# A streaming encoder layer: keys and queries projected first, attention laid between the gate's and u's projections, output weights asked for early

## The chip, the core and the metric

One core of one Trainium2 chip. The time is the device time of one execution in microseconds. The core's engines are TensorE (PE in the rows, matmuls; PEld is its weight load), VectorE (DVE), ScalarE (ACT), GpSimd (POOL) and SyncE (SP, which here only asks for weights). Each runs its own list of instructions in order, and they meet at semaphores.

## The reference

Two layers over 512 prompt rows and 64 sample rows, width 1024. Cut to what the change touches:

```python
h = x @ w_in                       # columns q 512 | k 128 | v 128 | u 512 | gv 512
q, k = rope(q, pos), rope(k, pos)
att_o = sink_attention(q, k, v, sinks, mask)            # window of 64-row chunks c-2, c-1, c
vn = layer_norm(gelu(gv)) per group; s = tril(w_s[g]) @ vn + b[g]
gm_o = gelu(u) * s                                      # over 128 positions, 4 groups
mixed = concat([rms_norm(att_o), rms_norm(gm_o)])
x = layer_norm(ALPHA * x + mixed @ w_o)
x = layer_norm(ALPHA * x + grouped_moe(x))              # 16 experts, top 2, for each row
```

## The kernel before, in words

All rows lie in five tiles of 128 (`NT = 5`; tile 4 is the sample, padded). Every large product is a sum of three passes, high part by high, high by low, low by high. A weight comes as a unit of 512 rows by 512 columns (1 MB; a unit of keys and values has 256 columns) into one of four slots of `raw`; ScalarE writes its high part (`split_hi`), VectorE the low part (`split_lo`), and a product waits for the latter. `unit s` stands in slot `s % 4`. The same pair of steps makes high and low parts of everything turned on TensorE: rows (`xt`), queries (`qt`), keys (`kt`), mixed rows (`mt`).

One layer runs: (1) the head: for each tile turn x, then project the gate's values gv; (2) projections of keys and values, of q, of u, each over all five tiles; (3) attention, gMLP and the product with w_o in a software pipeline over `t` (a loop of eight steps: scores of tile t, weighted values of tile t-1, the turn of mixed rows of t-2, output and layer norm of t-3); (4) the routing; (5) sixteen experts, whose weights stream at the pace of the DMA; (6) a tail that adds the experts' rows and normalises, within which the head of layer 1 stands. The layer loop turns behind that head.

The order is written out by hand, once for each engine. `fill_plan` (line 60) gives each PSUM result its bank and its turn in that bank; a writer waits (`wait_free`) until the turn before was read. `scores`, `gmlp`, `weighted_values`, `turn_mixed`, `output`, `turn_x1` are TensorE's steps; VectorE's are `rotate` (rope), `scores_out` (scale, mask, row maxima), `attention_out`, `gmlp_out`, `rms_norm`, `mixed_lo`, `mixed_out`, `layer_norm`; ScalarE's are `gelu`, `exponentials`, `probs_out` (copy of turned probabilities), `sums_of_squares`, `mixed_hi`, `router_rows_out`. A change of function on ScalarE between gelu, exp and sqrt brings an `ACT_TABLE_LOAD`.

Of the kernel before, what the change touches and what calls it, by code (L numbers as in the profile page):

```python
# [64 lines left out]
def fill_plan():  # L65
# [17 lines left out]
    fill(("qt", 0), "G")  # L83
    fill("kt1", "F")
    fill("wst", "H")
    for t in range(NT + 3):
        if t < NT:
            for j in range(4):
                fill(("s", t, j), "ABCD"[j])
        if t + 1 < NT:  # L90
            fill(("qt", t + 1), "H")
        if t == 0:
            for r in range(NT):
                fill(("gm", r), "GH"[r % 2])
        if 4 <= t < NT + 2:
            fill(("logit", t - 4), "H")
            fill(("turned logit", t - 4), "H")
        if t >= 3:
            for c in range(2):
                fill(("wo", c, t - 3), "AB"[c])  # L100
        if 1 <= t < NT + 1:
            for j in range(4):
                fill(("pt", t - 1, j), "EF"[j % 2])
            fill(("o", t - 1), "G")
        if 2 <= t < NT + 2:
            for h in range(2):
                fill(("mt", t - 2, h), "EF"[h])
        if 3 <= t < NT + 1:
            for h in range(2):
                fill(("rt", t - 3, h), "CD"[h])  # L110
    for t in (NT - 2, NT - 1):
# [14 lines left out]
def build(nc, x_prompt, x_sample, cache_k, cache_v, w_in, sinks, gm_ln_g, gm_ln_b, gm_ws, gm_bs,  # L126
# [5 lines left out]
    with ctx:  # L132
# [10 lines left out]

        raw = sb("raw", [P, RB, 4, HALF])
        w_hi = sb("w_hi", [P, RB, 4, HALF], F32R)
        w_lo = sb("w_lo", [P, RB, 4, HALF], F32R)
        x = sb("x", [P, NT, D])
# [7 lines left out]
        small = sb("small", [P, 400])  # L155
# [6 lines left out]
        xt_hi = over(base_t, "xt_hi", [P, KT_N, ROWS], F32R)  # L162
        xt_lo = over(base_t, "xt_lo", [P, KT_N, ROWS], F32R, 4 * KT_N * ROWS)
        keys_hi = over(base_t, "keys_hi", [P, 7 * P], F32R)
        keys_lo = over(base_t, "keys_lo", [P, 7 * P], F32R, at=3584)
        q_hi = over(base_t, "q_hi", [P, 4, P], F32R, at=7168)
        q_lo = over(base_t, "q_lo", [P, 4, P], F32R, at=9216)
        probs = over(base_t, "probs", [P, 2, 4, 2, 256], at=11264)
        probs_t = over(base_t, "probs_t", [P, 2, 4, P], at=27648)
        mask = over(base_t, "mask", [P, 3, 256], at=31744)  # L170
        ws_t = over(base_t, "ws_t", [P, 4, P], at=34816)
        consts = over(base_t, "consts", [P, 3 * P + 46 + 8 * NT])
        x1_t = over(base_t, "x1_t", [P, KT_N, P], at=36864)

        logits_t = over(base_t, "logits_t", [NE, P], at=3584)
# [9 lines left out]
        mt_hi = over(base_m, "mt_hi", [P, KT_N, P], F32R, at=2 * QB)  # L185
        mt_lo = over(base_m, "mt_lo", [P, KT_N, P], F32R, at=2 * QB + 4 * D)
        squares = over(base_m, "squares", [P, HALF], at=2 * QB + 8 * D)
# [31 lines left out]
        w12, warm = sm(NT, 2), sm(3)  # L219

# [19 lines left out]
        in_slot = over(base_t, "in_slot", [P, ON_CHIP, 2 * NT, P], BF16, at=11264)  # L240
# [32 lines left out]
        ws_in, mask_in, consts_in = sem("ws_in"), sem("mask_in"), sem("consts_in")  # L273
# [76 lines left out]
        def width(s):  # L350
            return 256 if s in (2, 3) else HALF
# [84 lines left out]
        def _(sp):  # L436
# [33 lines left out]
            with sp.Fori(0, DEPTH) as l:  # L470
                s = 0
                for c0, n in ((1280, HALF), (HALF, 256), (0, HALF), (768, HALF)):
# [3 lines left out]
                for c in range(2):  # L476
                    for k in range(2):
# [205 lines left out]
        def _(act):  # L683
# [24 lines left out]
            with act.Fori(0, DEPTH) as l:  # L708
# [6 lines left out]
                for t in range(4):  # L715
                    gelu(0, gv, t)
# [1144 lines left out]
```

## Time and profile before

| | us |
|---|---|
| median of three runs (1278.83 to 1288.0) | 1281.9 |
| profiled execution | 1284.19 |
| its span, first to last instruction | 1282.4 |
| granted TensorE clock, mean | 0.927 |
| PE busy in the span | 1062.2 (83%) |
| VectorE busy | 905.1 (71%) |
| ScalarE busy | 709.7 (55%) |

The profile's page cuts the span into 40 slices. TensorE's row of them shows nines for the projections (35 to 120 us, and 650 to 740 us in layer 1), sevens to nines in the attention stage, a gap at the routing, then nines through the experts, in which the DMA row also stands at nine. A "stretch" below is a span of time in this execution, in us from its start; "granted clock" 1.00 is 2.4 GHz and 0.5 is 1.2 GHz, so 0.97 says that 6% of the stretch ran at the lower level.

### The profile page before, as it was taken

Reading aid. Unit: us, or ns where it says so; the run is one execution under the profiler, and the core shown is the slowest. Engines: PE = TensorE matmul, PEld = TensorE weight load, DVE = VectorE, ACT = ScalarE, POOL = GpSimd, SP = SyncE. Lnnn points to the kernel's source line nnn. Section 1 sums busy time; section 2 is a strip of 40 time slices with the busy share of each in tenths; the row PEclk is TensorE's granted clock in tenths of the full one; section 3 lists DMA queues with packets and bytes.
Section 4 is the critical chain, followed back from the end, with each engine's and each line's share of the span. In section 5 each row is a group of like instructions: output and inputs, shape, how many; then the busy total and the mean of one; then the engine's idle time right before and its main releaser. Section 6 shows DMA issues by size and latency. Waiting matters only on the chain.

```text
span 1282.4 us, 16627 instructions
## 1 busy us (share of the span) xinstructions
PE 1062.2 (83%) x5422; PEld 875.3 (68%) x5422; DVE 905.1 (71%) x1096; ACT 709.7 (55%) x857; POOL 233.5 (18%) x164
## 2 busy tenths in 40 slices
PE   4999789947899999997389977996589999999920
PEld 3887677736777787785278856884477777777810
DVE  2573864568788888985758466636778788888827
ACT  2423663254777777776431267513468677777722
POOL 3000000007122211201440000000541222221015
PEclk9999999968999999999589988998689999999975
DMA  9422100026999999996713202102389999999751
GB/s 292 140 72 99 67 34 25 33 83 208 348 359 355 374 365 370 383 366 246 276 51 139 86 13 83 41 17 99 107 307 361 360 355 381 369 358 369 282 192 57
DMA packets 115620, 273.24 MB, mean 213 GB/s; under 512 B 10016, under 2 KB 13056, under 8 KB 114400
## 3 DMA queue, kind: packets, MB, share of 16 engines
q1 hardware_dynamic: 98608, 227.36, 49.8%
q0 software_dynamic: 14336, 33.00, 7.2%
q10 hardware_dynamic: 2608, 12.06, 2.6%
q8 instruction: 33, 0.54, 0.2%
q14 instruction: 35, 0.29, 0.1%
HBM read 262.00 MB, written 25.22 MB: 224 GB/s over the span
## 4 chain that ended last, share of the span: by engine, by line
PE 39%; DMA 17%; DVE 16%; issue 13%; ACT 8%; POOL 3%; DVEq 2%; POOLq 1%; ACTq 0%; SPq 0%
DMA raw<-in_w_gate 14%; PE bankA L1494 8%; PE bankB L1494 8%; DVE w_lo L385 5%; PE bankC L1494 4%; ACT w_hi L379 4%; PE bankD L1494 3%; PE bankA L1706 3%; PE bankB L1706 3%; POOL slot_rows L608 2%; DVE xt_lo L400 2%; PE bankC L1729 2%; DMA rows<-x_rows,cur_src 2%; PE bankD L1729 2%; PE bankE L1483 1%
## 5 line engine op out<-in xcount | busy, mean ns | idle before, releaser
L385 DVE TENSOR_TENSOR w_lo<-raw,w_hi 128x2048 fp32r<-128x2048 f32 x216 | 487.5, 2268 | 114.9 <-ACT w_hi L379 113.4
L379 ACT ACTIVATE w_hi<-raw 128x2048 fp32r<-128x2048 f32 x216 | 409.7, 1901 | 218.1 <-DMA raw<-in_w_down 60.9
L1706 PE MATMUL bankA<-w_hi,xt_hi 128*128 128x512 f32 x256 | 103.8, 405 | 18.8 <-DVE xt_lo L400 18.1
L1706 PE MATMUL bankB<-w_hi,xt_hi 128*128 128x512 f32 x256 | 102.8, 401 | 0.0
L1706 PE MATMUL bankA<-w_lo,xt_hi 128*128 128x512 f32 x256 | 101.0, 394 | 0.0
L1706 PE MATMUL bankA<-w_hi,xt_lo 128*128 128x512 f32 x256 | 100.9, 394 | 0.0
L1706 PE MATMUL bankB<-w_hi,xt_lo 128*128 128x512 f32 x256 | 100.1, 391 | 0.0
L1706 PE MATMUL bankB<-w_lo,xt_hi 128*128 128x512 f32 x256 | 99.7, 390 | 0.0
L594 POOL DMA_INDIRECT y_rows<-expert_out,idx x32 | 55.3, 1728 | 216.4 <-ACT expert_out L859 216.4
L588 POOL DMA_INDIRECT rows<-x_rows,idx x24 | 46.0, 1917 | 248.7 <-PE bankF L1483 233.0
L1706 PEld LDWEIGHTS bankA<-w_hi,xt_hi 128*128 128x128 f32 x256 | 48.8, 190 | 38.6 <-issue 29.2
L395 ACT ACTIVATE xt_hi<-bankE 128x512 fp32r<-128x512 f32 x42 | 24.6, 585 | 68.2 <-PE bankE L1483 68.2
L1729 PE MATMUL bankC<-w_hi,xt_hi 128*128 128x512 f32 x128 | 53.6, 419 | 3.8 <-DVE xt_lo L400 3.8
L1706 PEld LDWEIGHTS bankA<-w_hi,xt_lo 128*128 128x128 f32 x256 | 48.8, 190 | 10.6
L1706 PEld LDWEIGHTS bankB<-w_hi,xt_lo 128*128 128x128 f32 x256 | 48.0, 188 | 10.7
L1706 PEld LDWEIGHTS bankA<-w_lo,xt_hi 128*128 128x128 f32 x256 | 48.8, 191 | 9.4
L400 DVE TENSOR_TENSOR xt_lo<-bankE,xt_hi 128x512 fp32r<-128x512 f32 x42 | 28.8, 685 | 36.9 <-ACT xt_hi L395 36.9
L1706 PEld LDWEIGHTS bankB<-w_lo,xt_hi 128*128 128x128 f32 x256 | 48.2, 188 | 9.3
L1706 PEld LDWEIGHTS bankB<-w_hi,xt_hi 128*128 128x128 f32 x256 | 48.1, 188 | 9.1
L1729 PE MATMUL bankC<-w_hi,xt_lo 128*128 128x512 f32 x128 | 51.1, 399 | 0.0
L1729 PE MATMUL bankC<-w_lo,xt_hi 128*128 128x512 f32 x128 | 50.8, 397 | 0.0
L1729 PE MATMUL bankD<-w_hi,xt_hi 128*128 128x512 f32 x128 | 50.4, 394 | 0.0
(321 smaller groups left out, 2479.1 us busy)
## 6 DMA issues: line engine op xcount, KB each, us to landing
raw<-in_w_gate SPq DMA_DIRECT2D x64, 1024.0 KB, 8.1
raw<-in_w_up SPq DMA_DIRECT2D x64, 1024.0 KB, 7.8
raw<-in_w_down SPq DMA_DIRECT2D x64, 1024.0 KB, 7.3
raw<-in_w_in SPq DMA_DIRECT2D x12, 1024.0 KB, 8.0
raw<-in_w_o SPq DMA_DIRECT2D x8, 1024.0 KB, 5.3
y_rows<-y_rows ACTq DMA_DIRECT2D x8, 1024.0 KB, 8.3
x_rows<-x POOLq DMA_DIRECT2D x10, 512.0 KB, 3.0
raw<-in_w_in SPq DMA_DIRECT2D x4, 512.0 KB, 8.2
```

Source lines behind the costliest of these rows:

```text
L379: act.activation(w_hi[:, s % RB, :, 0:n], raw[:, s % RB, :, 0:n], ACT.Copy).then_inc(hi_done, 1)
L385: dve.tensor_tensor(w_lo[:, s % RB, :, 0:n], raw[:, s % RB, :, 0:n], w_hi[:, s % RB, :, 0:n].bitcast(F32), ALU.subtract).then_inc(lo_done, 1)
L395: act.activation(dst, bank_of(name)[:, :].rearrange("p (k n) -> p k n", k=4), ACT.Copy).then_inc(s, 1)
L400: read(dve.tensor_tensor(lo, bank_of(name)[:, :].rearrange("p (k n) -> p k n", k=4), hi.bitcast(F32), ALU.subtract), name)
L588: pool.indirect_dma_start(out=rows[:, e % 2, :], out_offset=None, in_=x1_dram, in_offset=bass.IndirectOffsetOnAxis(ap=src.bitcast(U32), ax ...
L594: pool.indirect_dma_start(out=y2_dram, out_offset=bass.IndirectOffsetOnAxis(ap=idx[:, e, 0:1].bitcast(U32), axis=0), in_=expert_out[:, e % ...
L608: pool.indirect_dma_start(out=slot_dram, out_offset=bass.IndirectOffsetOnAxis(ap=slots[:, c:c + 1].bitcast(U32), axis=0), in_=ints[:, c, : ...
L1483: ins = pe.transpose(bank_of(name)[:, k * P:(k + 1) * P], src, ident)
L1494: ins = pe.matmul(out, a[:, k, col:col + P], w[:, slot, j, 0:n], start=(m == 0 and a is a_hi and w is w_hi), stop=(m == len(steps) - 1 and ...
L1706: ins = pe.matmul(out, a[:, 4 * k + t, (c % 2) * P:(c % 2 + 1) * P], w[:, (s + k) % RB, t, :], start=(k == t == 0 and a is xt_hi and w is ...
L1729: ins = pe.matmul(bank_of(f"down{h}")[:, :], a[:, 2 * j + r, cols], w[:, (s + j) % RB, 2 * r + h, :], start=(j == r == 0 and a is xt_hi an ...
```

## The change

- `w_in` is taken in the order keys and values, q, gate, u. The head of each layer projects keys, values and q tile by tile (it projected gv before). The banks of these projections rotate over six (A, B, C, D, G, H).
- Each projection and each output product can be issued in two halves of four row blocks, so other work stands between them. In five rounds t = 0 to 4 TensorE does gate(t), scores(t), u(t), and the weighted values of tile t-1, in pieces (`half_product`, `turn_probs`, `values`). gMLP goes by tile, not by group: `gmlp(t)` are four 128-column products.
- ScalarE and VectorE get orders written out to match: gelu, exponentials and copies of probabilities alternate in each round; the spreads of the gate's norm come in three lots (`gate_spread`, `gate_scale`).
- Scratch moves: the turned x stays until its last projection; probabilities have a buffer for each tile (two lie in raw slots 0 and 1); queries and keys lie in raw slots 2 and 3; mixed rows have two buffers. So the units of `w_o` are asked for when their slot is free: units 8 and 9 behind the turns of tile 0's and tile 1's probabilities, 10 and 11 behind tile 4's scores.
- The mask shrinks to 8 numbers a row, fetched once by six small DMAs at the start instead of one of 393 KB in each layer.

```diff
-    for g in range(4):
-        for t in range(NT):
-            fill(("proj", g, t), "ABCD"[(g * NT + t) % 4])
+    for t in range(NT):
+        for g in range(2):
+            fill(("proj", g, t), "ABCDGH"[(2 * t + g) % 6])
...
+                for s, free in ((8, ("pt", 0, 3)), (9, ("pt", 1, 3)), (10, ("s", NT - 1, 3)), (11, ("s", NT - 1, 3))):
+                    wait_filled(sp, free, l)
...
+            for m in range(3):
+                for a in range(2):
+                    pool.dma_start(mask[:, m, 4 * a:4 * a + 4], c_mask[m, :, 0::64], allow_slow_non_contiguous=True).then_inc(boot, 16)
...
@@ ScalarE
+                for t in (2, 3):
+                    gelu(2, gv, t)
+                    probs_out(t - 1, range(4))
+                    gelu(3, u, t)
+                    queries_out(t + 1)
+                    exponentials(t)
+                    gate_spread(2 * t - 4, 2 * t - 2)
...
@@ VectorE
+                for t in range(NT):
+                    keys_out(t)
+                    if t == NT - 1:
+                        split_lo(dve, l, 4)
+                        split_lo(dve, l, 5)
+                    rotated_queries(t)
...
+                gmlp_out(0)
+                gmlp_out(1)
+                scores_out(4)
+                attention_out(2)
+                rms_norm(0)
+                split_lo(dve, l, 8)
+                rms_norm(1)
+                gate_scale(2, 4, 2)
+                gate_norm(2)
+                gate_norm(3)
+                mixed_lo(0)
+                split_lo(dve, l, 9)
...
+                gate_scale(4, NT, 3)
+                gate_norm(4)
+                attention_out(4)
+                rms_norm(2)
+                gmlp_out(4)
+                mixed_out(0)
+                layer_norm(0)
...
@@ TensorE, head
                 for t in range(NT):
-                    if 2 <= t + 1 < NT:
+                    wait_read(pe, ("xt", t, 1), l)
+                    for k in range(2):
+                        projection(l, 0, t, k)
+                    if t in (1, 2):
                         turn_rows(l, t + 1)
...
+                    for k in range(2):
+                        projection(l, 1, t, k)
+                    if t in (0, 2):
+
+                        turn_rows(l, 1 if t == 0 else 4)
...
@@ TensorE, rounds
+                            turn_probs(t - 1, (0, 1))
+                            projection(l, 3, t, 0)
+                            values(t - 1, 0)
+                            values(t - 1, 1)
+                            turn_probs(t - 1, (2, 3))
+                            if t == NT - 1:
+                                turn_mixed(0)
+                            projection(l, 3, t, 1)
+                            values(t - 1, 2)
+                            values(t - 1, 3)
...
+                output(0, 0)
+                gmlp(2)
+                gmlp(3)
+                attention_end(NT - 1)
+                turn_mixed(1)
+                output(0, 1)
+                gmlp(4)
+                for t in range(1, NT):
+                    output(t, 0)
+                    if t + 1 < NT:
+                        turn_mixed(t + 1)
```

First place, TensorE at the weighted values. Before, in tile 1's (bank E and F take turned probabilities, G the values; `kv` are keys and values, `probs_t` the turned probabilities):

```order
L1483 MATMUL bankE<-ident,probs 128x128 x4
L1537 REGISTER_ALU
L1483 MATMUL bankF<-ident,probs 128x128 x4
L324 REGISTER_ALU
L328 REGISTER_ALU
L1559 MATMUL bankG<-kv,probs_t 128x64 x4
L1537 REGISTER_ALU
L1483 MATMUL bankE<-ident,probs 128x128 x4
L1559 MATMUL bankG<-kv,probs_t 128x64 x4
L1537 REGISTER_ALU
L1483 MATMUL bankF<-ident,probs 128x128 x4
L328 REGISTER_ALU
```

After, in tile 2's (`probs_57` is that tile's buffer, bank B the product of u of tile 3, `xt` the turned rows):

```order
L1538 MATMUL bankB<-w_lo,xt 128x512
L1538 MATMUL bankB<-w_hi,xt 128x512
L332 REGISTER_ALU
L336 REGISTER_ALU
L1596 MATMUL bankG<-kv,probs_t 128x64 x8
L1577 REGISTER_ALU
L1525 MATMUL bankE<-ident,probs_57 128x128 x4
L1577 REGISTER_ALU
L1525 MATMUL bankF<-ident,probs_57 128x128 x4
L1538 MATMUL bankB<-w_hi,xt 128x512
L1538 MATMUL bankB<-w_lo,xt 128x512
```

A value product that stood right behind a turn now has half a projection of u ahead of it, and the next half behind it.

Second place, VectorE ahead of the first output product, which waits for the low part of tile 0's mixed rows (`mt_lo`, after: `mt_70`). Before:

```order
L1124 RECIPROCAL small<-small 128x2
L1127 SCALAR_TENSOR_TENSOR q<-q,small,table 128x512
L1127 SCALAR_TENSOR_TENSOR u<-u,small,table 128x512
L1074 REGISTER_ALU
L1075 TENSOR_TENSOR small<-small 128x8
L1077 RECIPROCAL small<-small 128x8
L320 REGISTER_ALU
L1080 TENSOR_TENSOR q<-bankG,small 128x512
L399 ISA
L400 TENSOR_TENSOR mt_lo<-bankE,mt_hi 128x512
L399 REGISTER_ALU
L400 TENSOR_TENSOR mt_lo<-bankF,mt_hi 128x512
```

After (`gv` rows are the gate's norm of tiles 2 and 3):

```order
L1131 SCALAR_TENSOR_TENSOR u<-u,small,table 128x512
L1081 RECIPROCAL small<-small 128x8
L1073 TENSOR_SCALAR gv<-gv,small 128x128 x4
L1075 TENSOR_TENSOR gv<-gv,table 128x512
L1077 TENSOR_TENSOR gv<-gv,table 128x512
L1073 TENSOR_SCALAR gv<-gv,small 128x128 x4
L1075 TENSOR_TENSOR gv<-gv,table 128x512
L1077 TENSOR_TENSOR gv<-gv,table 128x512
L407 ISA
L408 TENSOR_TENSOR mt_70<-bankE,mt_70 128x512
L407 REGISTER_ALU
L408 TENSOR_TENSOR mt_70<-bankF,mt_70 128x512
```

The low part stood behind an attention output; now it stands behind the gate's norm of two tiles, and a `w_lo` split stands a little further ahead.

Third place, VectorE behind the head. Before (the last low parts of turned x, then the statistics of gv; the branch is the layer loop's start):

```order
L400 TENSOR_TENSOR xt_lo<-bankE,xt_hi 128x4x128
L400 TENSOR_TENSOR xt_lo<-bankF,xt_hi 128x4x128
L400 TENSOR_TENSOR xt_lo<-bankE,xt_hi 128x4x128
L400 TENSOR_TENSOR xt_lo<-bankF,xt_hi 128x4x128
L385 TENSOR_TENSOR w_lo<-raw,w_hi 128x4x256 x2
L1027 UNCONDITIONAL_BRANCH
L1027 ISA
L1033 BN_STATS small<-gv 128x6 x16
```

After (keys, then queries, of tile 0; bank A and B are wanted again by the projections of tile 3):

```order
L408 TENSOR_TENSOR xt<-bankE,xt 128x512
L408 TENSOR_TENSOR xt<-bankF,xt 128x512
L408 TENSOR_TENSOR xt<-bankE,xt 128x512
L408 TENSOR_TENSOR xt<-bankF,xt 128x512
L1045 UNCONDITIONAL_BRANCH
L1045 ISA
L1050 COPY kv<-bankA 128x128
L1010 TENSOR_TENSOR rope_a<-bankA,rope 128x128
L1012 TENSOR_TENSOR rope_b<-bankA,rope 128x2x32
L1013 TENSOR_TENSOR rope_b<-bankA,rope 128x2x32
L1021 TENSOR_TENSOR kv<-rope_a,rope_b 128x128
L1010 TENSOR_TENSOR rope_a<-bankB,rope 128x512
```

The first reader of a projection's bank is now VectorE behind the last turned tile and behind the loop's start; it was ScalarE (gelu).

## Rows read from the trace of the kernel before

**Rows 1.** Stretches: length, busy time of each engine, then granted clock, DMA share, GB/s.

```profile
95.15:259.34 164.19, 146.47 (x867) 122.45 (x866) 92.19 (x152) 74.13 (x178) 4.56 (x8) 0.97 0.14 50
713.35:878.94 165.59, 147.05 (x868) 122.25 (x867) 92.02 (x152) 74.12 (x178) 4.57 (x8) 0.96 0.14 50
122.36:165.71 43.35, 30.33 (x232) 25.43 (x230) 32.68 (x53) 31.00 (x86) 0.74 (x1) 0.92 0.20 71
```

**Rows 2.** TensorE's waits, 95 to 262: us in total, times, longest.

```profile
PE bankG L1559 <- ACT probs_t L746: 5.3, 6, 4.0
```

**Rows 3.** TensorE in order of time, 53 to 80: start, us, operation.

```profile
53.53 0.28 PE L1494 MATMUL bankB<-w_hi,xt_hi 128*128 128x256 f32 x1
...
56.40 0.28 PE L1494 MATMUL bankC<-w_hi,xt_hi 128*128 128x256 f32 x1
...
67.92 0.40 PE L1494 MATMUL bankC<-w_hi,xt_hi 128*128 128x512 f32 x1
...
73.39 0.39 PE L1494 MATMUL bankD<-w_hi,xt_hi 128*128 128x512 f32 x1
```

**Rows 4.** TensorE, 152 to 208: as before, in brackets the idle time and its releaser.

```profile
152.70 1.20 PE L1559 MATMUL bankG<-kv,probs_t 128*128 128x64 f32 x8 [4.03 <-ACT probs_t L746]
...
186.47 0.38 PE L1577 MATMUL bankA<-keys_hi,q_hi 64*128 64x256 f32 x1
...
188.43 1.92 PE L1617 MATMUL bankH<-x_t,wrt 128*16 128x128 f32 x16
190.28 0.50 PE L1494 MATMUL bankA<-w_hi,mt_hi 128*128 128x512 f32 x1
...
201.59 0.65 PE L1483 MATMUL bankE<-ident,probs 128*128 128x128 f32 x4
...
207.39 0.61 PE L1483 MATMUL bankE<-ident,q 128*128 128x128 f32 x4
```

**Rows 5.** VectorE in order of time, 97 to 157.

```profile
97.40 1.11 DVE L1064 TENSOR_SCALAR gv<-gv,small 128x128 f32<-128x128 f32 x4
98.58 0.69 DVE L1066 TENSOR_TENSOR gv<-gv,table 128x512 f32<-128x512 f32 x1
...
99.96 4.49 DVE L385 TENSOR_TENSOR w_lo<-raw,w_hi 128x2048 fp32r<-128x2048 f32 x2
...
150.55 0.68 DVE L1093 SCALAR_TENSOR_TENSOR probs<-bankA,mask 128x512 f32<-128x512 f32 x1
...
153.12 2.29 DVE L1098 TENSOR_REDUCE small<-probs 128x8 f32<-128x2048 f32 x1
...
156.72 0.75 DVE L1127 SCALAR_TENSOR_TENSOR q<-q,small,table 128x512 f32<-128x512 f32 x1
```

**Rows 6.** ScalarE in order of time, 157 to 175.

```profile
157.20 0.60 ACT L746 ACTIVATE probs_t<-bankF 128x512 f32<-128x512 f32 x1 [1.82 <-PE bankF L1483]
157.81 1.28 ACT L753 ACT_TABLE_LOAD   x1
...
170.42 0.51 ACT L753 ACTIVATE probs<-probs,small 128x256 f32<-128x256 f32 x1 [1.37 <-DVE small L1103]
...
174.38 0.19 ACT L755 ACTIVATE small<-small 128x8 f32<-128x8 f32 x1
```

**Rows 7.** TensorE, the first projection of layer 0.

```profile
18.95 0.77 PE L1494 MATMUL bankA<-w_hi,xt_hi 128*128 128x512 f32 x1 [11.70 <-issue]
```

**Rows 8.** TensorE, the head of layer 1.

```profile
629.70 0.79 PE L1494 MATMUL bankA<-w_hi,xt_hi 128*128 128x512 f32 x1 [6.05 <-DVE xt_lo L400]
...
645.05 1.11 PE L1483 MATMUL bankE<-ident,x 128*128 128x128 f32 x4 [5.95 <-POOL x L668]
```

**Rows 9.** ScalarE at the turn of the layer loop.

```profile
664.21 1.28 ACT L712 ACT_TABLE_LOAD   x1 [3.02 <-issue]
```

**Rows 10.** GpSimd, the small strided fetch of the gMLP bias.

```profile
26.84 0.75 POOL L551 DMA_DIRECT2D small<-in_gm_bs  x1
```

**Rows 11.** The page, its DMA issues: times asked for, size, us to landing.

```profile
raw<-in_w_o SPq DMA_DIRECT2D x8, 1024.0 KB, 5.3
```

More of the change, by code:

```diff
@@ new lines, in _ @@
+                gelu(3, u, 1)
+                probs_out(0, range(4))
+                queries_out(2)
+                exponentials(1)
+                for t in (2, 3):
[5 more added lines that the diff above has]
+                    gate_spread(2 * t - 4, 2 * t - 2)
+                sums_of_squares(0)
+                sums_of_squares(1)
+                probs_out(3, range(2))
@@ new lines, in _ @@
+                split_hi(act, l, 8)
+                gelu(2, gv, 4)
+                probs_out(3, range(2, 4))
+                mixed_hi(0)
+                split_hi(act, l, 9)
+                gelu(3, u, 4)
+                split_hi(act, l, 10)
+                exponentials(4)
+                split_hi(act, l, 11)
+                probs_out(4, range(4))
+                mixed_hi(1)
+                gate_spread(4, NT)
+                sums_of_squares(2)
+                sums_of_squares(3)
+                row_spread(0)
@@ new lines, in _ @@
+                gate_stats(0)
+                scores_out(0)
+                queries_lo_out(1)
+                for t in range(1, 4):
+                    scores_out(t)
+                    if t >= 2:
+                        attention_out(t - 2)
+                    gate_stats(t)
+                    if t == 3:
+                        gate_scale(0, 2, 1)
+                        gate_norm(0)
+                        gate_norm(1)
+                    queries_lo_out(t + 1)
+                gmlp_out(0)
@@ new lines, in _ @@
+                gmlp_out(1)
[9 more added lines that the diff above has]
+                split_lo(dve, l, 9)
+                gate_stats(4)
+                attention_out(3)
+                split_lo(dve, l, 10)
+                gmlp_out(2)
+                gmlp_out(3)
@@ new lines, in _ @@
+                split_lo(dve, l, 11)
+                mixed_lo(1)
+                gate_scale(4, NT, 3)
[5 more added lines that the diff above has]
+                layer_norm(0)
+                mixed_lo(2)
+                rms_norm(3)
+                mixed_out(1)
+                layer_norm(1)
+                mixed_lo(3)
+                expert_logits_out(0)
+                rms_norm(4)
@@ L1213, in _ @@
+                mixed_out(2)
+                logits_out(0)
+                layer_norm(2)
+                mixed_lo(4)
+                expert_logits_out(1)
+                mixed_out(3)
+                logits_out(1)
+                layer_norm(3)
+                expert_logits_out(2)
+                mixed_out(4)
+                logits_out(2)
+                layer_norm(4)
                 expert_logits_out(NT - 2)
@@ new lines, in _ @@
+                gmlp(2)
[4 more added lines that the diff above has]
+                gmlp(4)
+                for t in range(1, NT):
+                    output(t, 0)
+                    if t + 1 < NT:
+                        turn_mixed(t + 1)
+                    if t >= 2:
+                        expert_logits(t - 2)
+                    output(t, 1)
+                    turn_x1(t - 1)
+                    if t >= 2:
+                        turn_logits(t - 2)
@@ L1764, in turned, with three_pass @@
                         ins.then_inc(ov_pe, 1)
-                    def three_pass(out, col, units, after):
+                    def three_pass(out, n, units, after):
                         pe.wait_ge(ov_dve, ran * DVE_STEPS + after)
```

522 lines of the change are left out of this document (233 added, 289 removed).

## The prediction

> **What bounds the kernel now.** I read the slices of the page first: the experts run at the DMA's pace and are not touched, so what a layer gains ahead of its routing is passed on to the end. Then, by stretches, the part of each layer from the first projection of u (95.15; 713.35) to the end of tile 4's output product (259.34; 878.94). In the first, 164.2 us, PE is busy 146.5 and idle 17.7; the granted clock is 0.97, so 0.03 x 164.2 = 4.9 us of its work went to the lower level, and the work at 2.4 GHz is 141.6. In layer 1: 165.6, idle 18.5, 0.04 x 165.6 = 6.6 lost, work 140.4 [rows 1]. VectorE has 92 and ScalarE 74 us there. So PE has the most work, but it is not continuous: in the stretch 122 to 166, behind the projections, it is busy 30.3 of 43.4 at clock 0.92 [rows 1], because scores, row maxima, exponentials, copies and values follow each other with nothing laid between. The waits say whose: 5.3 us of them are for the copies of probabilities, one alone 4.0 [rows 2]. The view in order of time shows PE idle 4.03 us ahead of tile 1's values [rows 4]. About 22.6 and 25.1 us a layer (idle and clock) are all that this part can give.
>
> **The change, part by part.** I follow each engine's new list with durations of before. Prices: half a projection 5.47 / 2 = 2.7; keys and values of a tile 2.9 [rows 3]; scores of a tile 1.96, router product 1.85, values of a tile with their four turns 5.8, of which a pair of turns 0.9 [rows 4]; VectorE: the gate's norm of a tile 1.1 + 2 x 0.76 = 2.7, a weight's low part 2.25, scores out 4 x 0.6 + 2.3 + 0.6 = 5.3, `rms_norm` 1.6 [rows 5]; ScalarE: table load 1.28, exponentials of a tile 174.38 + 0.19 - 170.42 = 4.15, a copy 0.6 [rows 6]. Time 0 is the start of gate(0).
>
> *Round 0*, to 14.9. ScalarE must write the keys' high parts behind unit 7's low part (7.1); scores(0) start at 9.8, as PE arrives. No stall.
>
> *Round 1*, to 34.7. scores(1) wait for the low part of queries 1, which VectorE has behind scores_out(0) and its maxima: 1.4 us. The values of tile 0 still stand right behind their turns, and the copies behind the gelu of u(1): 2.4. Sum 3.8.
>
> *Rounds 2 and 3*, to 53.4 and 73.9 (with two gMLP products). Here the idea works: turned probabilities are copied while half a u projection runs (first place in the order). The tight chain is ScalarE's behind `turn_queries`: copy 0.6, load and exp 5.4, load and sqrt 1.6, load and gelu 1.9, two copies 1.1 = 10.6, against PE's 2.7 + 1.0 + 2.7 + 1.0 + 0.9 + 2.7 = 11.0 ahead of the values. It holds by 0.4, so I take no stall.
>
> *Round 4*, to 94.6. `turn_mixed(0)` needs a bank that ScalarE empties behind a weight split (1.9) and a gelu with its load (1.9): stall 1.6.
>
> *First output product.* It needs tile 0's low mixed rows. VectorE does scores_out(4) to 85.0, attention_out 1.1, rms_norm 1.7, a weight 2.3, rms_norm 1.7, the norm of two tiles 5.6, then mixed_lo: done 98.7 (second place). Stall 4.2. Tile 4's values follow with 1.2 of stall.
>
> *Second output product of tile 1's row.* `output(1, 0)` wants bank A, which mixed_out(0) reads behind gate_norm(4), attention_out(4), rms_norm(2), gmlp_out(4): VectorE gets there at 123.7, PE at 120.2. Stall 3.5. From there PE needs 5.5 + 0.9 + 1.9 + 5.5 + 0.9 + 0.2 = 14.9 a tile and VectorE about 11, so PE sets the pace to the end.
>
> Stalls together 3.8 + 1.6 + 4.2 + 1.2 + 3.5 = 14.3, less 0.6 where a piece's modelled end already covers them: 13.7. The work is 141.6 + 5 x 5.47 for gv = 168.9 in layer 0 and 167.7 in layer 1. On the clock's loss: it was 4.9 for 17.7 idle, 6.6 for 18.5; in proportion 3.8 and 4.9. My stalls are mostly shorter and stand between long products, so I take 2 and 3; the proportional value is the other end. Adding full pieces one by one gives 2 to 3 us less work than the busy time (its ends overlap); I take 2 off. New part: 168.9 + 13.7 + 2 - 2 = 182.6, and 182.4. Before, with gv: 164.2 + 27.3 = 191.5, and 192.9. Gains 8.9 and 10.5.
>
> *Heads.* Before, layer 0 went from 18.95 [rows 7] to 95.15. The first keys unit has half the bytes and half the splitting, so PE starts near 11; but q(0) needs units 2 and 3, 3 MB in rather than 2, and ends near 25. Then comes what the change adds: keys of tile 3 want bank A, which VectorE reads behind the low part of tile 4's x (third place): 2.6 us. By steps of 8.35 a tile, u would start at 94.0 instead of 95.15: gain 1. Bounds -3 to +5. Layer 1 is now paced by the tail: PE waits 6.05 and 5.95 for rows [rows 8], and q(0) fills the second wait (+5); but q(2)'s turn of tile 4, then the loop's start, for which ScalarE needed 3.0 us [rows 9], stand ahead of the keys' read: stall 4.7 and some clock. Result -1, bounds -5 to +4. Together 0.
>
> *At the end of the part* VectorE copies a turned logit ahead of the last layer norm, which waits for PE's turns behind the last product: 0.6 a layer, 1.2.
>
> *Weights of w_o.* Units 10 and 11 are asked for at 81, split from 94 and 101 on ScalarE, used from 113; such a unit lands in 5.3 us [rows 11]. Cover of some 8 us; were it gone, each us would be one of PE. Experts' first units are asked for from 90 on and used 90 us later. *Mask.* Six strided fetches like the gMLP bias, 0.75 us of issue each [rows 10], 4.5 on POOL ahead of releasing x tiles 2 to 4; turn_rows(2) stands near 31 and the release near 26. Nothing. Layouts, mask by broadcast, buffers: the same element counts, nothing (bounds +-1).
>
> Sum: -8.9 - 10.5 + 0 + 1.2 = -18.2. I have counted only the waits I could see in five lists, and a list followed misses waits, never work; for those I add 2 us a layer (one more wait like those for queries). So -14.2. The profiled execution took 1284.2, of which 1282.4 is its span; the median of the runs is 2.3 below it, 1281.9. The change is the same against each, so the span goes to 1268.2, the profiled execution to 1270.0 and the median to **1268**.
>
> **A rule weighed against the trace.** In each round ScalarE changes between gelu, exp and sqrt, up to three loads, where before one tile had at most two. The rows show a load of 1.28 us that starts 0.01 us behind the copy ahead of it [rows 6]: nothing else is paid. The Trainium skill (ScalarE: Activation LUTs, What ACT_TABLE_LOAD costs) states about 2.66 us for a switch, with a drain. By the rule the chain of rounds 2 to 4 would grow by 3 x 1.38 = 4.1 and stand 3.7 over PE's; three rounds, two layers: +22, so about 1290. It is part of rival 3.
>
> **Rivals.**
> 1. *The hand-offs are hidden better.* The 4.2 and 3.5 stalls shrink (VectorE can gain on me wherever I let it wait), no clock is lost and nothing unseen comes. Gain 8.9 + 10.5 + about 4 a layer + heads 3 = 30: 1252. For it: VectorE's 92 us of 165. Against: VectorE works through from 81 to 124 in my list without a gap.
> 2. *VectorE's queue is later than I have it.* Both stalls double (+7.7 a layer): it decides if one of the four weight splits there waits for ScalarE, whose exp(4) stands between them. 1268 + 15 = 1283: no change.
> 3. *Slower: ScalarE paces the rounds.* Place: probs_out behind exp, sqrt and gelu. Price: if its chain is 3.5 us longer than 10.6 (late maxima, or the rule above), PE stalls 3.1 in rounds 2, 3, 4 of both layers, 19 us, and after such waits it ran values at the lower clock before (1.20 for eight, [rows 4]): 1.5 each, 9. That is 1268 + 28 = 1296. It decides from about 3 us on. Against: loads show no drain, and maxima are ready 5 us ahead of exp.
>
> **How the numbers follow.** Forecast 0.45, its own range 1260 to 1276; rival 1 0.24; rival 2 0.19; rival 3 0.12 (0.03 of it the rule). 1% of 1281.9, about what can be told from no change here, is 12.8: faster means under 1269.1. Of the forecast's range a little over half lies below. Faster: 0.25 + 0.24 = 0.49; same 0.20 + 0.19 = 0.39; slower 0.12. The range leaves out 0.08 of rival 1's low end and all of rival 3: 1249 to 1286.
>
> **What would show it.** Right: no PE wait for `probs_t` over 1 us in rounds 2 and 3; a wait of about 4 us for `mt` low parts ahead of the first output product and of 3 to 4 for bank A; about 182 us from gate(0) to tile 4's last output in both layers; a wait of 2 to 6 us in the fourth tile of each head. Wrong: waits for probabilities in every round (rival 3); experts that don't start earlier by what the part gains.

## The result, and the profile after

The changed kernel takes 1290.95 us (median of 20 runs) beside 1282.95 for the kernel before: ratio 1.0061, interval 1.0041 to 1.0080. It is slower by 0.6%; I had forecast 1268, and 1286 as the upper end of the range. The profiled execution took 1288.56, its span 1287.0, granted clock 0.924.

The stretches of the changed kernel that answer to [rows 1] start at the first projection of gate(0), since the gate now belongs to this part (columns: length, busy time of each engine with the number of instructions, granted clock, DMA share, GB/s). The first two are the parts of the two layers, the next four lie inside the first part, the last two in the head of layer 1:

```profile
65.26:260.82 195.56, 181.22 (x1010) 150.04 (x1011) 116.64 (x233) 88.49 (x192) 5.32 (x10) 0.96 0.18 63
692.54:885.43 192.89, 178.30 (x1010) 147.40 (x1011) 115.04 (x233) 88.46 (x192) 4.57 (x8) 0.96 0.18 63
126.91:135.30 8.39, 8.39 (x51) 6.56 (x50) 2.23 (x4) 8.03 (x22) 0.00 (x0) 1.00 0.00 0
142.45:151.56 9.11, 9.11 (x59) 8.34 (x58) 5.23 (x14) 3.28 (x5) 0.00 (x0) 0.81 0.00 0
177.29:184.39 7.10, 7.10 (x26) 5.80 (x27) 6.29 (x13) 6.00 (x19) 0.00 (x0) 0.79 0.42 148
202.98:210.38 7.40, 7.40 (x26) 5.88 (x27) 5.47 (x8) 0.29 (x1) 0.48 (x1) 0.77 0.24 73
630.87:692.54 61.67, 52.54 (x273) 46.84 (x273) 41.35 (x74) 17.95 (x20) 23.04 (x21) 0.86 0.20 64
673.20:678.68 5.48, 5.48 (x25) 5.48 (x26) 4.74 (x14) 0.00 (x0) 0.00 (x0) 0.51 0.00 0
```

I predicted 182.6 and 182.4 for the first two; they are 195.6 and 192.9. The idle time in them, 14.3 and 14.6, is close to my 13.7. The busy time is not.

TensorE's waits in layer 0's part (total, times, longest), which answer to [rows 2]:

```profile
PE bankG L1596 <- DVE q L1092: 4.4, 3, 1.5
PE bankA L1538 <- DVE x L1140: 3.2, 1, 3.2
PE bankC L1615 <- DVE q_lo L408: 2.6, 2, 1.3
PE bankA L1538 <- DVE mt L408: 2.0, 1, 2.0
PE bankE L1525 <- ACT ws_t L802: 1.2, 1, 1.2
PE bankG L1596 <- ACT probs_t L737: 1.0, 4, 0.2
```

What the change was to remove is removed: the wait for copied probabilities was 5.3 with one of 4.0, and is 1.0 in four pieces. The largest wait is one that stands nowhere in my prediction. TensorE, then VectorE, in round 3 of the changed kernel in order of time (start, us, operation, in brackets the idle time and its releaser):

```profile
140.62 1.99 PE L1596 MATMUL bankG<-kv,probs_t 128*128 128x64 f32 x16 [1.47 <-DVE q L1092]
```

```profile
136.44 2.29 DVE L1108 TENSOR_REDUCE small<-probs 128x8 f32<-128x2048 f32 x1
...
139.45 0.20 DVE L1089 RECIPROCAL small<-small 128x8 f32<-128x8 f32 x1
139.80 0.69 DVE L1092 TENSOR_TENSOR q<-bankG,small 128x512 f32<-128x512 f32 x1
```

The values of tile 2 go to bank G, which still holds those of tile 1. Its reader, `attention_out(1)`, stands on VectorE behind `scores_out(3)` with its row maxima (2.29 us), and ends at 140.5. This happens in rounds 2, 3 and 4, with waits of 1.48, 1.47 and 1.46.

### The profile page after: what moved, and what is told of

It reads as the page before. It is cut to its first block, busy times and chain, and to the rows that moved or that the text cites. A ratio compares the mean times of both kernels' runs of the same rounds, so it can differ in the third digit from the quotient of the medians.

```text
span 1287.0 us, 17033 instructions
## 1 busy us (share of the span) xinstructions
PE 1074.2 (83%) x5470; PEld 885.9 (69%) x5470; DVE 909.9 (71%) x1124; ACT 717.4 (56%) x865; POOL 242.5 (19%) x170
## 4 chain that ended last, share of the span: by engine, by line
PE 33%; DMA 21%; DVE 20%; issue 12%; ACT 6%; DVEq 3%; POOL 2%; POOLq 1%; ACTq 1%; SPq 0%
DMA raw<-in_w_gate 16%; PE bankA L1538 9%; DVE w_lo L393 7%; PE bankB L1538 7%; ACT w_hi L387 5%; DVE xt L408 3%; PE bankG L1596 2%; DVE small L1108 1%; PE bankE L1525 1%; PE bankD L1538 1%; DVE x L1464 1%; PE bankC L1799 1%; POOL slot_rows L621 1%; PE bankA L1776 1%; PE bankD L1799 1%
## 5 line engine op out<-in xcount | busy, mean ns | idle before, releaser
L393 DVE TENSOR_TENSOR w_lo<-raw,w_hi 128x2048 fp32r<-128x2048 f32 (+1 forms) x216 | 487.8, 2268 | 107.9 <-ACT w_hi L387 106.7
L387 ACT ACTIVATE w_hi<-raw 128x2048 fp32r<-128x2048 f32 (+1 forms) x216 | 409.8, 1901 | 179.8 <-DMA raw<-in_w_gate 60.3
L1776 PE MATMUL bankA<-w_hi,xt 128*128 128x512 f32 x512 | 167.6, 398 | 22.1 <-DVE xt L408 22.1
L1776 PE MATMUL bankB<-w_hi,xt 128*128 128x512 f32 x512 | 166.3, 396 | 0.0
L1776 PEld LDWEIGHTS bankA<-w_hi,xt 128*128 128x128 f32 x512 | 97.0, 189 | 52.4 <-issue 32.6
L1776 PEld LDWEIGHTS bankB<-w_hi,xt 128*128 128x128 f32 x512 | 96.2, 188 | 19.5
L1776 PE MATMUL bankA<-w_lo,xt 128*128 128x512 f32 x256 | 100.3, 392 | 0.0
L1776 PE MATMUL bankB<-w_lo,xt 128*128 128x512 f32 x256 | 99.8, 390 | 0.0
L1799 PE MATMUL bankC<-w_hi,xt 128*128 128x512 f32 x256 | 93.6, 407 | 3.3 <-DVE xt L408 3.3
L1799 PE MATMUL bankD<-w_hi,xt 128*128 128x512 f32 x256 | 90.0, 392 | 0.0
L1538 PE MATMUL bankB<-w_hi,xt 128*128 128x512 f32 x224 | 75.9, 404 | 1.5 <-DVE w_lo L393 1.4
L1538 PEld LDWEIGHTS bankA<-w_hi,xt 128*128 128x128 f32 x224 | 46.1, 218 | 26.0 <-issue 10.0
```

The costliest lines, as they stand in the source:

```text
L387: act.activation(w_hi[:, s % RB, :, 0:n], raw[:, s % RB, :, 0:n], ACT.Copy).then_inc(hi_done, 1)
L393: dve.tensor_tensor(w_lo[:, s % RB, :, 0:n], raw[:, s % RB, :, 0:n], w_hi[:, s % RB, :, 0:n].bitcast(F32), ALU.subtract).then_inc(lo_done, 1)
L1538: ins = pe.matmul(bank_of(name)[:, 0:n], part[:, 4 * k0 + j, :], w[:, s % RB, j, 0:n], start=(k0 == j == 0 and part is hi and w is w_hi), ...
L1776: ins = pe.matmul(out, a[:, c % 2, 4 * k + t, :], w[:, (s + k) % RB, t, :], start=(k == t == 0 and a is xt_hi and w is w_hi), stop=(k == 1 ...
L1799: ins = pe.matmul(bank_of(f"down{h}")[:, :], a[:, n, 2 * j + r, :], w[:, (s + j) % RB, 2 * r + h, :], start=(j == r == 0 and a is xt_hi an ...
```

## Experiments

Each kernel is the changed one with the edit shown. The results, with the span of the profiled execution cut at the same places: start of gate(0) in layer 0, end of tile 4's output product, the first turned x of layer 1 ("head 1" is from there to gate(0) of layer 1), and the output product of layer 1. "Busy" is TensorE's in that part, "end" the time from layer 1's last output product to the end of the span.

| kernel | ratio to before | gate(0) | part 0 / busy | head 1 | part 1 / busy | end |
|---|---|---|---|---|---|---|
| before | 1 | 67.9* | 191.5* | 64.4* | 192.9* | 403.5 |
| changed | 1.0061 (1.0041 to 1.0080) | 65.3 | 195.6 / 181.2 | 68.8 | 192.9 / 178.3 | 401.6 |
| e_oread | 0.9970 (0.9943 to 0.9997) | 65.1 | 186.3 / 174.3 | 66.9 | 188.5 / 177.8 | 398.1 |
| e_mix | 0.9928 (0.9893 to 0.9962) | 65.9 | 184.9 / 174.8 | 66.7 | 183.7 / 174.8 | 400.4 |
| e_head | 1.0013 (0.9978 to 1.0047) | 62.8 | 192.5 / 179.4 | 63.1 | 193.2 / 178.5 | 403.1 |
| e_quarter | 1.0263 (1.0211 to 1.0315) | 67.0 | 202.1 / 186.3 | 67.2 | 206.2 / 190.9 | 395.1 |
| e_all | 0.9788 (0.9747 to 0.9828) | 62.6 | 177.2 / 172.3 | 63.4 | 178.7 / 172.4 | 404.9 |
| e_best | 0.9677 (0.9644 to 0.9711) | 63.3 | 173.3 / 171.8 | 64.7 | 174.3 / 171.9 | 399.6 |
| e_best_q | 0.9757 (0.9727 to 0.9787) | 62.2 | 180.0 / 178.2 | 63.8 | 180.3 / 178.4 | 399.7 |
| e_best_undo | 0.9797 (0.9751 to 0.9843) | 63.5 | 178.5 / 172.6 | 63.0 | 183.4 / 177.3 | 403.7 |

\* with the 27.3 us of the gate's projections counted into the part instead of the head, as in the prediction. The last column is the same code in the changed kernel and all its edits, and yet it goes from 395 to 405 in single executions. The way from the end of part 0 to the first turned x of layer 1, which has no column, goes from 361 to 367 (362 before, 363 in the changed kernel). So I read each edit in its own part and take the total from the ratio. A difference from the changed kernel is the quotient of two ratios, and the interval of e_head touches that of the changed kernel. A part's busy time is that of one execution, which need not be a typical one: that of e_oread took 1267.7 us at a mean clock of 0.930, beside a median of 1278.0 and clocks of 0.923 to 0.927 in the other nine.

### e_oread: the reader of bank G first

```diff
                 for t in range(1, 4):
-                    scores_out(t)
                     if t >= 2:
                         attention_out(t - 2)
+                    scores_out(t)
...
-                scores_out(4)
                 attention_out(2)
+                scores_out(4)
```

> The changed kernel with one thing moved on VectorE: attention_out(t-2) stands ahead of scores_out(t) instead of behind it, for t = 2, 3 and 4. Nothing else. Theory A (waits that my lists missed, and the lower clock behind short waits): in the changed kernel TensorE waits 3 times 1.46 us a layer for the reader of bank G, and the stretch from that wait of round 3 to round 4 ran at a granted clock of 0.81. Gone with the wait: 4.4 of idle and about 2 of clock a layer, so 1291 - 13 = 1278, and the page shows no wait of bank G for q. Theory B (the rounds are paced by VectorE and ScalarE anyway): the wait comes back at another bank in the same round, 1288 to 1291. Theory C (only the idle time comes back, the clock does not): 1291 - 9 = 1282.

Measured: 0.9% less than the changed kernel, about 12 us. No wait for `q` is left, part 0 is 9.3 shorter and part 1 4.4. Theory A holds for the total. The layers show something else as well: busy time falls by 6.9 in layer 0 and by 0.5 in layer 1, with the same instructions, and the wait ahead of the first output product grows from 2.0 to 3.8, since TensorE comes earlier and VectorE does not. How much of the 6.9 belongs to the edit and how much to this execution, whose clock was the highest of the ten, one trace does not tell. Here too the product behind that wait ran at a granted clock of 0.77:

```profile
169.29:176.65 7.36, 7.36 (x26) 5.91 (x27) 6.29 (x13) 4.21 (x12) 0.00 (x0) 0.77 0.39 142
```

### e_mix: VectorE's list around the first output products

```diff
                 gate_norm(2)
-                gate_norm(3)
                 mixed_lo(0)
                 split_lo(dve, l, 9)
+                gate_norm(3)
...
                 split_lo(dve, l, 11)
+                mixed_out(0, (0,))
                 mixed_lo(1)
...
-                mixed_out(0)
+                mixed_out(0, (1,))
                 layer_norm(0)
```

> The changed kernel with VectorE's list changed around the first output products: mixed_lo(0) and the low part of unit 9 stand ahead of gate_norm(3) instead of behind it, and the first half of mixed_out(0), which frees bank A, stands ahead of mixed_lo(1) instead of behind gate_norm(4), attention_out(4), rms_norm(2) and gmlp_out(4). Theory A: the two waits of 2.0 and 3.2 us a layer vanish, and the two output products behind them take 5.7 us each instead of 7.1 and 7.4 (8.0 and 8.3 in layer 1), since they no longer follow a gap: 5.2 + 3.1 = 8.3 in layer 0, 9.7 in layer 1, so 1291 - 18 = 1273. Theory B (VectorE is the limit there): the time is wanted again at gmlp_out, mixed_lo(1) or layer_norm(0), and less than 8 us come back in all: 1283 to 1290.

Measured: 1.3% less than the changed kernel, 17 us; theory A said 18. Of the two waits 0.7 is left of the first and nothing of the second in layer 0, and the output products behind them take 5.7 us:

```profile
PE bankG L1597 <- DVE q L1092: 4.4, 3, 1.5
...
PE bankA L1539 <- DVE mt L408: 0.7, 1, 0.7
```

### e_head: turned rows one product earlier

```diff
                     if t in (1, 2):
-                        turn_rows(l, t + 1)
+                        turn_rows(l, 2 * t)
                     for k in range(2):
                         projection(l, 1, t, k)
-                    if t in (0, 2):
+                    if t in (0, 1):
 
-                        turn_rows(l, 1 if t == 0 else 4)
+                        turn_rows(l, 2 * t + 1)
```

> The changed kernel with TensorE's head changed: tile 3's rows are turned behind q(1) and tile 4's behind keys and values of tile 2, each one product earlier, so that VectorE is through with the turned rows and the loop's start one product earlier. Theory A: in layer 1 the wait of 5.7 us ahead of keys and values of tile 3 goes to 0 to 1, and the products behind it no longer run at a clock of 0.5 (about 2.7 us); in layer 0 the wait of 2.3 goes. Sum 5.2 + 2.7 + 2.3 = 10: 1291 - 10 = 1281. Theory B (the loop's start, some 3.4 us on VectorE and ScalarE, and the rows of the tail set the pace): the wait moves to the turn of tile 4 or to q(3), and no more than 4 come back: 1287 to 1291.

Measured: 0.5% less, 6 us, between the theories, and hardly clear of the noise. The wait ahead of keys and values of tile 3 was, in the changed kernel, TensorE's and VectorE's:

```profile
673.20 0.58 PE L1538 MATMUL bankA<-w_hi,xt 128*128 128x256 f32 x1 [5.73 <-DVE rope_b L1013]
```

```profile
668.30 0.68 DVE L408 TENSOR_TENSOR xt<-bankF,xt 128x512 fp32r<-128x512 f32 x1
672.39 0.29 DVE L1050 COPY kv<-bankA 128x128 f32<-128x128 f32 x1 [3.41 <-issue]
```

With the rows turned earlier 2.1 us of the 5.7 stay. VectorE has the turned rows behind it at 658.83, 6.6 us earlier than in the changed kernel if one counts from the first turned x, but then it stands 5.25 us at the start of the layer loop instead of 3.41, and what it waits for there the trace does not show:

```profile
664.08 0.29 DVE L1050 COPY kv<-bankA 128x128 f32<-128x128 f32 x1 [5.25 <-issue]
```

Head 1 is 5.7 shorter, head 0 2.4: the place is right, 8 of the expected 10 us are seen in the trace, 6 in the ratio.

### e_quarter: the gate's projection in quarters, scores in blocks of six

```diff
-                    projection(l, 2, t, 0)
                     if t:
-                        scores(t, (0, 1))
-                    projection(l, 2, t, 1)
+                        for k in range(2):
+                            projection(l, 2, t, k, (0, 1))
+                            scores(t, (2 * k,))
+                            projection(l, 2, t, k, (2, 3))
+                            scores(t, (2 * k + 1,))
```

> The changed kernel with more changes between work, not more work: in rounds 1 to 4 the gate's projection goes in quarters, and behind each quarter stand the scores of one pair of heads, so that scores come in four blocks of 6 products instead of two of 12. The same products, banks and waits. Read from the changed kernel: between two products of a projection 0.23 us pass, from the last one to the first scores product 0.32, between the first two scores products 0.22 instead of 0.11, from the last to the next projection product 0.21, between that one and its successor 0.31 to 0.34: some 0.4 us for going into a block of scores and out again. Theory A (the change of work costs): 2 more blocks in 4 rounds of 2 layers, 16 x 0.4 = 6.4 us more of TensorE's busy time; 1291 + 6 = 1297. Theory B (the excess over my sum is the clock alone): within 1 us of the changed kernel, 1290 to 1292.

Measured: 2.0% above the changed kernel, 26 us; I had expected 6. My price of a cut was too low. The same round 3, at full clock in both, took 8.39 in the changed kernel (above) and here

```profile
130.37:140.46 10.09, 9.99 (x51) 7.24 (x50) 2.77 (x4) 9.49 (x23) 0.00 (x0) 1.00 0.01 2
```

so 1.70 for two cuts. How it comes about shows in the order of time; the changed kernel, round 3, at the edge between half a projection and a pair of scores:

```profile
129.31 0.39 PE L1538 MATMUL bankA<-w_lo,xt 128*128 128x512 f32 x1
129.53 0.39 PE L1538 MATMUL bankA<-w_hi,xt 128*128 128x512 f32 x1
129.85 0.38 PE L1615 MATMUL bankC<-keys_hi,q_hi 64*128 64x256 f32 x1
130.07 0.28 PE L1615 MATMUL bankC<-keys_lo,q_hi 64*128 64x256 f32 x1
130.19 0.28 PE L1615 MATMUL bankC<-keys_hi,q_lo 64*128 64x256 f32 x1
130.20 0.38 PE L1615 MATMUL bankD<-keys_hi,q_hi 64*128 64x256 f32 x1
...
130.89 0.28 PE L1615 MATMUL bankD<-keys_hi,q_lo 64*128 64x256 f32 x1
131.10 0.50 PE L1538 MATMUL bankA<-w_hi,xt 128*128 128x512 f32 x1
131.44 0.39 PE L1538 MATMUL bankA<-w_lo,xt 128*128 128x512 f32 x1
```

And a block of six in e_quarter, with the product behind it:

```profile
132.10 0.38 PE L1617 MATMUL bankC<-keys_hi,q_hi 64*128 64x256 f32 x1
...
133.00 0.50 PE L1538 MATMUL bankA<-w_hi,xt 128*128 128x512 f32 x1
```

Starts inside the projection are 0.23 apart; at the edges 0.32, 0.22, 0.21 and 0.34. And scores in 64 rows of one bank run beside those of the other (starts 0.01 apart), the second 0.35 behind the first: 12 products in a pair take 1.25, 24 in one block took 1.96 before [rows 4], but 6 alone take 0.9. So the edit does more than cut: a block of six fills one bank and has nothing beside it. Four such blocks take 3.6 where two of twelve take 2.5, which is 1.1 of the 1.70; the other 0.6 is edges. Part 0 grew by 6.5, the size of the added work (6.4, from e_best_q below), part 1 by 13.3, of which 12.6 is busy time: the same 6.4 and about 6 of clock. The two spans differ by only 15 us: the end is 6.5 shorter in this execution, which took 1304.0 where the median of its six runs is 1313.1. Where the rest of the 26 lies no trace shows.

### e_all, e_best: the edits together

e_all is the three edits above. e_best adds the following (`scores_out(0, 1)` takes the low part of queries 1 between tile 0's scores and their maxima):

```diff
@@ VectorE
                 rms_norm(1)
+                mixed_lo(0)
+                split_lo(dve, l, 9)
                 gate_scale(2, 4, 2)
                 gate_norm(2)
-                mixed_lo(0)
-                split_lo(dve, l, 9)
                 gate_norm(3)
-                gate_stats(4)
                 attention_out(3)
+                gate_stats(4)
...
-                scores_out(0)
-                queries_lo_out(1)
+                scores_out(0, 1)
@@ ScalarE
+                probs_out(0, range(2))
                 gelu(3, u, 1)
-                probs_out(0, range(4))
+                probs_out(0, range(2, 4))
@@ TensorE, attention_end(0)
+                    turn_probs(t, (0, 1))
                     if t == 0:
                         wait_read(pe, "wst", l)
                         pe.sem_inc(held_pe, 1)
-                    turn_probs(t, (0, 1))
```

> The three edits together: attention_out ahead of scores_out, mixed_lo(0) and half of mixed_out(0) earlier, rows of tiles 3 and 4 turned one product earlier. Alone they stood at 0.997, 0.993 and 1.001 of the kernel before, against 1.006 of the changed kernel. Theory A (independent waits at different places of one path): the gains of 0.9, 1.3 and 0.5% add up, less about 1.2 us a layer, because without the waits for bank G TensorE comes 4 us earlier to the first output product while VectorE does not (with the first edit alone that wait grew from 2.0 to 3.8): 0.979 + 0.002 = 0.981, about 1259. Theory B (a second limit, the DMA ahead of the experts or VectorE's 92 us in the part, takes over): 0.988 or more, no better than the best single edit by over half a per cent.

> As e_all, and five more moves: mixed_lo(0) and the low part of unit 9 right behind rms_norm(1), ahead of the gate's norm of tiles 2 and 3; attention_out(3) ahead of gate_stats(4); the low part of queries 1 ahead of the maxima of tile 0's scores; on ScalarE two copies of tile 0's probabilities ahead of the gelu of u(1); on TensorE the wait for the spatial weights' copy behind the first turned probabilities. Theory A: the wait ahead of the first output product goes to under 0.5 us (VectorE would be through at the time TensorE arrives), the wait for the low part of queries 1 (1.3) and most of that for ws_t (1.2) go: 1.2 + 1.3 + 0.7 = 3.2 a layer, so 6 us under e_all, 0.976 of the kernel before, about 1252. The two layer parts from gate(0) to tile 4's last output product then take about 180 us each, a little under the 182.6 that I predicted of the changed kernel. Theory B: gate_norm(2) or (3) come too late for gmlp(2) and gmlp(3), and the wait only moves there: no better than e_all.

Measured: e_all 0.979 (expected 0.981), e_best 0.968 (expected 0.976, 1252), at 1241.92 us. The three edits of e_all add up (0.9, 1.3 and 0.5% alone, 2.7% together), so within the noise their waits were independent. The parts of e_best, the two layers, then round 3 and the first output product:

```profile
63.28:236.62 173.34, 171.82 (x1011) 143.95 (x1010) 114.77 (x233) 88.26 (x192) 4.56 (x8) 1.00 0.21 70
666.98:841.28 174.30, 171.90 (x1011) 143.97 (x1010) 115.73 (x233) 88.27 (x192) 4.71 (x9) 1.00 0.20 70
117.59:125.98 8.39, 8.39 (x52) 6.56 (x50) 3.20 (x7) 8.03 (x22) 0.00 (x0) 1.00 0.01 3
159.49:165.23 5.74, 5.74 (x28) 4.76 (x28) 5.37 (x14) 5.71 (x17) 0.00 (x0) 1.00 0.64 208
```

TensorE is busy 171.8 of 173.3 us at full clock. This is the same work as in the changed kernel, where it took 181.2: the difference, 9.4 us, I put down to the lower clock. The granted clock of 0.96 over 195.6 us gives 7.8, and of 0.96 over 192.9 us in layer 1 7.7 where the busy times differ by 6.4, so it is most of the difference, to some 1.5 us. All that TensorE still waits for in part 0:

```profile
PE bankG L1599 <- ACT probs_t L737: 1.3, 4, 0.5
PE bankE L1528 <- ACT probs_t L737: 0.3, 1, 0.3
```

By the parts e_best gains 3.9 and 4.4 on e_all, 8 us for a forecast of 6. The other 5 of the 13 us between the medians I can't place: of the 11.4 us between the two profiled spans 5.2 lie in the end, where the code is the same, and e_all's runs spread over 12 us. Nor do I know the share of each of the five moves, which were not run apart.

### e_best_q and e_best_undo: one thing put back

e_best_q is e_best with e_quarter's edit; e_best_undo is e_best without e_oread's.

> The kernel of e_best with the gate's projection in quarters and the scores in four blocks, as in e_quarter. It tells the price of the cuts from that of the waits they met: e_quarter cost 26 us over the changed kernel where I had forecast 6. Read from e_quarter, round 3 from the first gate product to the first turn of probabilities: 10.09 us against 8.39 with halves. Theory A (the cuts themselves cost 1.70 a round, the rest of the 26 came from waits and from the lower clock behind them): 8 rounds x 1.70 = 13.6, and 1 us a layer in round 1, where the first quarter ends before the low part of queries 1: 1242 + 15 = 1257. Theory B (every cut costs more than the rows show, or the clock falls by itself in such a mix): 1242 + 24 = 1266 or more.

> The kernel of e_best with one thing put back: attention_out(t-2) behind scores_out(t), with its maxima, for t = 2, 3, 4, as in the changed kernel. Theory A (that place alone costs three waits of 1.46 a layer at bank G, and the clock behind short waits falls only sometimes): 2 x 4.4 = 8.8, with clock up to 13: 1251 to 1255, and VectorE's list is no later than before at the first output product. Theory B (in the kernel with all other waits gone the gap is taken up elsewhere): under 4 us, 1242 to 1246.

Measured, e_best_q: 0.8% above e_best, 10 us by the ratio, 6.7 and 6.0 by the parts (expected 15). The clock stays at 1.00 in both:

```profile
62.23:242.23 180.00, 178.18 (x1011) 146.66 (x1010) 115.45 (x233) 88.49 (x192) 4.56 (x8) 1.00 0.21 67
673.41:853.69 180.28, 178.35 (x1010) 146.78 (x1011) 115.72 (x233) 88.46 (x192) 4.57 (x8) 1.00 0.20 67
```

So e_quarter's edit costs 178.2 - 171.8 = 6.4 a layer, 1.6 a round, with no loss of clock; theory B falls.

Measured, e_best_undo: 1.2% above e_best, 15 us (expected 9 to 13). Parts and TensorE's waits in layer 0:

```profile
63.45:241.96 178.51, 172.58 (x1011) 143.70 (x1010) 114.90 (x233) 88.26 (x192) 4.56 (x8) 1.00 0.20 68
669.65:853.07 183.42, 177.30 (x1011) 147.95 (x1010) 115.50 (x233) 88.50 (x192) 4.57 (x8) 0.97 0.20 66
```

```profile
PE bankG L1599 <- DVE q L1093: 4.4, 3, 1.5
PE bankG L1599 <- ACT probs_t L737: 1.3, 4, 0.5
```

The three waits of 1.47 are back in both layers and cost 4.4 in each. In layer 0 they went with 0.8 more in busy time, in layer 1 with 5.4, for the same three waits, in one execution. By the parts it is 5.2 + 9.1 = 14.3; I had allowed up to 4 for the clock, and it came to 6.

## Why the prediction was wrong

The step that failed is the price of laying attention between the projections. I took the cut work at 2 us less than the uncut, the clock's loss at 2 and 3, and rounds 2 and 3 without a stall; the runs showed 2.9 and 4.2 more work, 9.4 and 6.4 for the clock, and a stall of 1.5 in each of rounds 2, 3 and 4. Beside the kernel before, with its gate counted in, layer 0's part has 3.4 less idle time (17.7, 14.3), 2.9 more work (168.9, 171.8) and about 4.5 more lost to the clock (4.9, 9.4): 4 us longer. In layer 1 3.9 less idle time stand against 4.2 more work, and it comes out even. The head of layer 1 adds 4.4.

Term by term the sum failed in three places of the layer part and one of the head. Against the forecast span of 1268.2 the measured one, 1287.0, is 18.8 longer: part 0 +13.0, part 1 +10.5, head 1 +3.4, head 0 -1.5, the end -2.5 and the way between 0, and -4 for the 2 us a layer that I had set aside for unseen waits.

**The work: 168.9 - 2 and 167.7 - 2.** Measured 171.8 and 171.9 (e_best). 4.9 and 6.2 short. I priced half a projection at 5.47 / 2 and half of a tile's scores at 1.96 / 2, and then took 2 us off for ends that overlap. Cutting gives nothing back: a round of gate and scores takes 8.39 instead of 5.47 + 1.96 = 7.43, 0.96 more, and five rounds make 4.8. The rows for it were in the trace of before: scores start at 186.47 and end at 188.43, with a router product of whole width behind [rows 4]; I divided the number instead of looking at its edges. Of the 0.96, two blocks of twelve for one of 24 make 2 x 1.25 - 1.96 = 0.54; the other 0.42 is at the edges.

**The clock: 2 and 3.** Measured 9.4 and 6.4 (181.2 - 171.8; 178.3 - 171.9; 7.8 and 7.7 by the granted clock). Even my other end, in proportion to idle time (3.8 and 4.9), is less. I wrote that short stalls between long products would cost little. In layer 0 the 9.4 went with 14.3 us idle: behind waits of 1.96 and 3.15 the output products took 7.1 and 7.4 at 0.79 and 0.77 (near half of the time at 1.2 GHz) instead of 5.74.

**The stalls: 13.7.** Measured 14.3 and 14.6, but this is luck. "Rounds 2 and 3 ... no stall" is wrong: 1.48 and 1.47, and 1.46 in round 4, all for `attention_out`. I followed the tight chain of ScalarE, which held as I said, and forgot that the next values need the last ones read. Round 0 had a wait of 1.3 for the low part of queries 0 where I had none. In return round 1 cost 3.0 instead of 3.8, `turn_mixed(0)` nothing instead of 1.6, the first output product 2.0 instead of 4.2 and tile 4's values 0.5 instead of 1.2; bank A 3.2 for 3.5 was right, mechanism and place. The 2 us a layer for unseen waits was a third of what they came to in layer 0 (4.4 and 1.3).

**The heads.** Tile 3's keys waited for bank A in both layers as I said, 2.3 (2.6) and 5.7 (4.7). Layer 0's head gained 2.6 (predicted 1). Layer 1's lost 4.4 in its own length (predicted 1): the wait was 1 longer, and the products behind it and behind the wait at 645 ran partly or wholly at the lower level of 1.2 GHz; the one behind the 5.7 took 5.48 at 0.51, 2.6 us more than at full clock, which "some clock" did not cover.

**The rivals.** The kernel got slower and not faster, and the measured time lies between rivals 2 and 3. *VectorE's queue is later* (1283) is the nearest in kind: all the large waits of the part are VectorE's. But it came at another place, by order and not by amount, and none of them was doubled. *ScalarE paces the rounds* (1296) is refuted: waits for `probs_t` are 1.0 us in all, and 1.2 are for its copy of the spatial weights. The load between a copy and an exponential takes what it took before, ScalarE of the changed kernel in round 4:

```profile
150.05 0.60 ACT L732 ACTIVATE q_hi<-bankH 128x512 fp32r<-128x512 f32 x1 [1.58 <-PE bankH L1525]
150.67 1.28 ACT L744 ACT_TABLE_LOAD   x1
151.96 0.51 ACT L744 ACTIVATE probs<-probs,small 128x256 f32<-128x256 f32 x1
```

0.02 us stand ahead of the load and 0.01 behind it. The 2.66 us for a switch that the Trainium skill states (ScalarE: Activation LUTs, What ACT_TABLE_LOAD costs) are not seen here; the rows were right to go by. That the 1290 of that rule lies next to the measured 1291 is chance: none of the waits that it stands for is there. One row I misread in this rival: eight values in 1.20 us are hardly a sign of the lower clock, since eight take 1.15 at a granted clock of 1.00 in the changed kernel (102.05 to 103.20). *The hand-offs are hidden better* (1252, gain 30) did not come by itself, but with VectorE's list mended nearly all idle time and clock loss go, and the kernel takes 1242 although the cut work is dearer than I had it.

**Right:** units of w_o were never waited for, the mask cost nothing that shows, the experts start later or earlier by what the parts lose or gain, to some 5 us, and the logit's copy cost 0.4 (3.26 instead of 2.86 ahead of the last turn).

## What to carry to other kernels

In this kernel interleaving two chains on TensorE paid only once the readers of its PSUM banks stood early in VectorE's list: walk through the lists once per bank and ask who reads it last, not only who fills what is read. Price a piece of cut work at its edges and not as a fraction of the whole. And count a wait of 1.5 to 3 us between long products at up to about twice its length (4.4 us of waits came with 5.4 of clock in e_best_undo's layer 1, and with 0.8 in its layer 0), since the clock behind it may fall.

## What the runs showed of the hardware

- The clock lost behind idle time is not in proportion to it, and not even. The same three waits of 1.47 in e_best_undo went with 0.8 us more busy time in layer 0 and 5.4 in layer 1; a wait of 3.2 ahead of output(1, 0) was followed by 7.40 at clock 0.77 in the changed kernel and by 5.77 in e_oread; the two waits of 1.21 ahead of the first output product in e_all came in parts at clock 1.00. With 1.5 to 6.3 us idle in a part of 173 to 180 (e_best, e_best_q, e_all) the clock was 1.00, and with 6.1 in layer 1 of e_best_undo 0.97. The mean clock also differs between runs of one kernel (e_oread 0.923 to 0.930, e_best_undo 0.927 to 0.934). What decides between these cases stays open.
- Scores with 64 rows in two banks, each from its own half of the rows, run side by side: 24 products in 1.96 us, 12 in 1.25, 6 in 0.9. Cutting such a block of 24 in two costs 0.54, and each edge against a product of 128 rows some 0.1 to 0.2 more.
- At the start of the layer loop VectorE stands 3.4 us in the changed kernel (ScalarE 2.4, and 3.0 before, [rows 9]), and the bank that its first reader frees is held as long. It is no fixed time: with the last rows turned one product earlier VectorE stood 5.25 us in e_head and 4.95 in e_best. The cause is not shown.
